# Expert lookup of a PEER layer: sixteen row dots move from VectorE to TensorE, and the expert V rows are split differently

## What is computed

```python
qc = (xc @ w_query).reshape(C, 8, 2, 128)
s = einsum('chpd,hpnd->chpn', qc, sub_keys)          # 128 keys per half
top_s, top_i = top_k(s, 16)
cand_s = top_s[..., 0, :, None] + top_s[..., 1, None, :]
cand_i = top_i[..., 0, :, None] * 128 + top_i[..., 1, None, :]
best_s, best_pos = top_k(cand_s, 16)                 # 16 experts per token and head
expert_idx = take_along_axis(cand_i, best_pos)
g = softmax(best_s)
act = gelu(einsum('chkd,cd->chk', expert_u[expert_idx], xc))
out = einsum('chk,chkd->cd', g * act, expert_v[expert_idx])
```

## Time and profile before

| | us |
|---|---|
| median of three runs | 1690.85 (1689.32 to 1690.89) |
| the profiled execution | 1694.34 |
| its span in the trace | 1692.5 |
| DVE, PE, POOL, ACT busy | 1298.5, 1234.9, 842.8, 460.9 |
| DMA, mean over the span | 340 GB/s |

### The profile page before, as it was taken

One profiled execution on the slowest core, in us unless ns is written; L12 is line 12 of the kernel. 1 busy time (PEld: TensorE's weight loads), 2 busy tenths in 40 slices (PEclk: granted clock), 3 DMA queues, 4 the chain that ended last, 5 costly groups with the idle time before them and its releaser, 6 DMA issues.

```text
span 1692.5 us, 14464 instructions
## 1 busy us (share of the span) xinstructions
PE 1234.9 (73%) x4812; PEld 839.8 (50%) x4812; DVE 1298.5 (77%) x1802; ACT 460.9 (27%) x1023; POOL 842.8 (50%) x546
## 2 busy tenths in 40 slices
PE   9999999999995554001344544454699999999993
PEld 7888887778984343000122322332365555555551
DVE  5554666466699999999999999999796665666667
ACT  5333443554200100000135565552381000000000
POOL 1000010000174888877888888888565443444444
PEclk9999999999997778555666676666699999999997
DMA  8886546348799999999999999999899999999998
GB/s 237 223 207 196 169 143 213 99 148 278 260 410 415 422 411 396 385 371 362 395 382 407 403 413 387 398 401 422 335 313 380 410 409 411 410 410 409 410 409 347
DMA packets 150230, 575.81 MB, mean 340 GB/s; under 512 B 15586, under 2 KB 28596, under 8 KB 117268
## 3 DMA queue, kind: packets, MB, share of 16 engines
q0 software_dynamic: 74384, 421.30, 62.6%
q1 hardware_dynamic: 75460, 152.82, 26.9%
q10 hardware_dynamic: 320, 0.86, 0.1%
HBM read 572.57 MB, written 2.36 MB: 340 GB/s over the span
## 4 chain that ended last, share of the span: by engine, by line
PE 30%; DVE 28%; DMA 24%; POOL 12%; issue 4%; ACT 2%; DVEq 0%; ACTq 0%; POOLq 0%
DMA v_rows<-in_peer_expert_v,pick_row 21%; DVE big L1549 10%; DVE more_rows L1549 8%; PE ps L1692 6%; PE ps L1694 6%; PE ps L1693 6%; POOL big L691 5%; PE ps L2095 4%; POOL more_rows L691 3%; DVE big L1597 3%; POOL v_rows L671 3%; DMA more_rows<-in_peer_expert_u,pick_row 2%; PE ps L2118 1%; DMA big<-in_peer_expert_u,pick_row 1%; DVE big L1574 1%
## 5 line engine op out<-in xcount | busy, mean ns | idle before, releaser
L671 POOL DMA_INDIRECT v_rows<-in_peer_expert_v,pick_row x256 | 307.8, 1202 | 271.7 <-DVE big L1597 234.9
L1597 DVE SCALAR_TENSOR_TENSOR big<-v_rows,pick_w,big 128x1152 f32<-128x1152 f32 x203 | 287.6, 1417 | 151.7 <-DMA v_rows<-in_peer_expert_v,pick_row 149.7
L2095 PE MATMUL ps<-v_rows,diag 128*128 128x512 f32 (+1 forms) x312 | 182.9, 746 | 269.5 <-DMA v_rows<-in_peer_expert_v,pick_row 169.8
L1549 DVE CUSTOM_DVE_ANT_0 big<-big 128x2048 f32<-128x2048 f32 x150 | 340.1, 2283 | 12.9 <-DMA big<-in_peer_expert_u,pick_row 12.5
L691 POOL DMA_INDIRECT big<-in_peer_expert_u,pick_row x150 | 288.8, 1925 | 65.6 <-issue 43.2
L2095 PEld LDWEIGHTS ps<-v_rows,diag 128*128 128x128 f32 x312 | 83.3, 285 | 368.2 <-issue 194.8
L691 POOL DMA_INDIRECT more_rows<-in_peer_expert_u,pick_row x106 | 222.7, 2101 | 75.3 <-issue 28.3
L1030 DVE TENSOR_TENSOR split_lo<-raw,split_hi 128x1024 fp32r<-128x1024 f32 x119 | 145.8, 1225 | 143.7 <-ACT split_hi L719 118.1
L1549 DVE CUSTOM_DVE_ANT_0 more_rows<-more_rows,big 128x2048 f32<-128x2048 f32 x106 | 240.8, 2284 | 11.0 <-DMA more_rows<-in_peer_expert_u,pick_row 11.0
L2127 PE MATMUL ps<-big,dense 128*128 128x512 f32 (+1 forms) x512 | 213.5, 539 | 0.3 <-DMA big<-in_peer_expert_v 0.3
L2127 PE MATMUL ps<-big 128*128 128x512 f32 (+1 forms) x512 | 213.4, 539 | 0.0
(11 more groups left out here) (281 smaller groups left out, 1495.2 us busy)
## 6 DMA issues: line engine op xcount, KB each, us to landing
big<-in_peer_expert_v SPq DMA_DIRECT2D x128, 448.0 KB, 6.8
raw<-in_w_in SPq DMA_DIRECT2D x88, 512.0 KB, 3.7
raw<-in_w_out SPq DMA_DIRECT2D x32, 512.0 KB, 5.1
big<-in_peer_w_query SPq DMA_DIRECT2D x16, 512.0 KB, 6.5
raw<-in_peer_w_query SPq DMA_DIRECT2D x8, 512.0 KB, 7.6
spare<-in_peer_w_query SPq DMA_DIRECT2D x8, 512.0 KB, 8.3
v_rows<-in_peer_expert_v,pick_row POOLq DMA_INDIRECT x256, 14.2
big<-in_peer_expert_u,pick_row POOLq DMA_INDIRECT x150, 9.1
```

Source lines behind the costliest of these rows:

```text
L671: pool.indirect_dma_start(v_row(k), None, v_table, bass.IndirectOffsetOnAxis(pick_row[:, k:k + 1], 0)).then_inc(v_gathered[v_place(k)], 16)
L1549: dve.tensor_tensor_reduce(row, row, XN[:, place_of(m // TOPK)[0], :], 1.0, 0.0, ALU.mult, ALU.add, pick_dot[:, m:m + 1]).then_inc(dotted, 1)
L1597: dve.scalar_tensor_tensor(out=v, in0=row, scalar=pick_w[:, k:k + 1], in1=v, op0=ALU.mult, op1=ALU.add).then_inc(added, 1)
L2095: ins = pe.matmul(psf[:, c:c + w], diag[:, j % DIAGS, :], row[:, c:c + w], start=k == 0, stop=j == pe_adds(PICKS) - 1)
```

## The change

1. **Dots on PE.** Of head steps 1 to 8, the picks k = 4 and k = 10 (`TURNED_DOTS`: 20, 26, 36, 42, ..., 132, 138) are not dotted by DVE. PE turns the row, 16 blocks of 128 x 128, in four groups into two PSUM banks; ACT copies each group into one SBUF buffer (that of the four diagonals, which aren't needed yet); PE multiplies each block with the token columns already turned (`x1t`), into a 128 x 128 square in PSUM. Its diagonal holds the dots. DVE takes it with a product with the identity and a sum over 128 columns (`take_dot`), behind the dot of pick m + 4. The order in which `dotted` counts changes with it (`DOT_ORDER`, `dots_until`). The ring place of such a row is free when it has been turned.
2. **V beside the picks.** `V_FROM` 144 and every third pick, so that row 0 comes at pick 146 in POOL's, ACT's and PE's loops; 37 rows. ACT makes the diagonal ahead of the one-hots of the same m. The ring goes to six places at pick 138.
3. **Columns.** 1088 per gathered V row, 960 in the dense pass (512 + 448 per product pair).
4. **Scores** are made at k = 13 for head steps of the first eight, k = 9 behind them.
5. Small ones: two PSUM banks swapped for the groups, waits that guard PSUM and the diagonal buffer, and four private semaphores replaced by the engine's step counter.

```diff
-U_WIDE = 108
+U_WIDE = 138
-V_ROW = 1152
+V_ROW = 1088
-V_FROM, V_BESIDE = 112, 36
+V_FROM, V_BESIDE = 144, 37
+TURNED_DOTS = [n * TOPK + k for n in range(1, NH + 1) for k in (4, 10)]
+TAKEN_AFTER = 4
+SCORES_AT = (13, 9)
+DOT_GROUPS = 4
+DOT_ORDER = [f for m in range(PICKS) for f in ([m] if m not in TURNED_DOTS else []) + ([m - TAKEN_AFTER] if m - TAKEN_AFTER in TURNED_DOTS else [])]
+DOT_PLACE = {f: i for i, f in enumerate(DOT_ORDER)}
+def dots_until(m):
+    return DOT_PLACE[m] + 1
 def v_until(m):
-    return max(0, m - V_FROM + 1) // 4
+    return max(0, m - V_FROM + 1) // 3
...
                 f = before_in_place(m)
-                if f >= 0:
-                    pool.wait_ge(dotted, f + 1)
+                if f in TURNED_DOTS:
+                    pool.wait_ge(row_turned, DOT_GROUPS * (TURNED_DOTS.index(f) + 1))
+                elif f >= 0:
+                    pool.wait_ge(dotted, dots_until(f))
...
+            def turned_copies(q):
+                for g in range(q * DOT_GROUPS, (q + 1) * DOT_GROUPS):
+                    act.wait_ge(row_turned, g + 1)
+                    if g:
+                        act.wait_ge(turned_used, g)
+                    act.activation(turned_rows.rearrange("p c n -> p (c n)"), ps[:, g % 2, :], ACT.Copy).then_inc(turned_here, 1)
...
+                if m in TURNED_DOTS:
+                    turned_copies(TURNED_DOTS.index(m))
...
+                for p in v_at(m):
+                    pick_diag(p)
                 i = group_at(m)
...
-                for p in v_at(m):
-                    pick_diag(p)
...
+            def take_dot(m):
+                q = TURNED_DOTS.index(m)
+                dve.wait_ge(turned_used, DOT_GROUPS * (q + 1))
+                dots = ps[:, 2 + q % 2, 0:P]
+                dve.tensor_tensor_reduce(dots, dots, ident[:, :], 1.0, 0.0, ALU.mult, ALU.add, pick_dot[:, m:m + 1]).then_inc(dotted, 1)
...
-                pick_dot_of(m)
+                if m not in TURNED_DOTS:
+                    pick_dot_of(m)
+                if m - TAKEN_AFTER in TURNED_DOTS:
+                    take_dot(m - TAKEN_AFTER)
...
+            def turned_dot(m):
+                q, t = TURNED_DOTS.index(m), place_of(m // TOPK)[0]
+                row = row_here(pe, m)
...
+                def turn(c):
+                    g = q * DOT_GROUPS + c
+                    if g >= 2:
+                        pe.wait_ge(turned_here, g - 1)
+                    for j in range(KC // DOT_GROUPS):
+                        k = c * DOT_GROUPS + j
+                        ins = pe.transpose(ps[:, g % 2, j * P:(j + 1) * P], row[:, k * P:(k + 1) * P], ident[:, :])
+                    ins.then_inc(row_turned, 1)
+                def add(c):
+                    if c == 0 and q >= 2:
+                        pe.wait_ge(dotted, dots_until(TURNED_DOTS[q - 2]))
+                    pe.wait_ge(turned_here, q * DOT_GROUPS + c + 1)
+                    for j in range(KC // DOT_GROUPS):
+                        k = c * DOT_GROUPS + j
+                        ins = pe.matmul(ps[:, 2 + q % 2, 0:P], turned_rows[:, j, :], x1t[:, k, t * P:(t + 1) * P], start=k == 0, stop=k == KC - 1)
+                    ins.then_inc(turned_used, 1)
+                turn(0)
+                for c in range(1, DOT_GROUPS):
+                    turn(c)
+                    add(c - 1)
+                add(DOT_GROUPS - 1)
...
-                if k == TOPK - 1 and n + 2 < HEADS:
+                if k == SCORES_AT[n // NH] and n + 2 < HEADS:
                     head_scores(n + 2)
...
                 i = group_at(m - 2)
                 if i is not None:
                     group(0, i)
+                if m in TURNED_DOTS:
+                    turned_dot(m)
```

More of the change, by code:

```diff
@@ L414, in layer @@
         query_used = sem("query_used")
+        row_turned, turned_here, turned_used = sem("row_turned"), sem("turned_here"), sem("turned_used")
+        turned_rows = diag[:, :, :]
+        ALL_TURNED = DOT_GROUPS * len(TURNED_DOTS)
         def query_name(n):
@@ L940, in hot_first @@
                     v = hot0[:, 1, j, :]
-                    act.activation(v, iota[:, :], ACT.Square, bias=picks_t[:, 1, token:token + 1], scale=-1.0).then_inc(sem("hot_squared"), 1)
-                    act.wait_ge(sem("hot_squared"), token + 1)
+                    link(act.activation(v, iota[:, :], ACT.Square, bias=picks_t[:, 1, token:token + 1], scale=-1.0))
                     act.activation(v, v, ACT.Relu, bias=1.0, scale=-1.0).then_inc(sem("hot_act"), 1)
@@ L960, in group_out @@
                 act.wait_ge(token_made, t * P + (i + 1) * GROUP_TOKENS)
+                if t == 0 and i == 0:
+                    act.wait_ge(turned_used, ALL_TURNED)
                 act.activation(dense_w[t][:, :, i * GROUP_TOKENS:(i + 1) * GROUP_TOKENS],
-                               ps[:, 3 + i % 2, :].rearrange("p (j a) -> p a j", j=GROUP_TOKENS), ACT.Copy).then_inc(group_moved, 1)
+                               ps[:, 4 - i % 2, :].rearrange("p (j a) -> p a j", j=GROUP_TOKENS), ACT.Copy).then_inc(group_moved, 1)
+            def turned_copies(q):
[4 more added lines that the diff above has]
+                    act.activation(turned_rows.rearrange("p c n -> p (c n)"), ps[:, g % 2, :], ACT.Copy).then_inc(turned_here, 1)
             for m in range(PICKS):
@@ L1006, in _ @@
             v = slice(V_ROW, V_ROW + CHUNK)
-            act.activation(X[:, 1, v], ps[:, 6, :], ACT.Copy).then_inc(sem("dense_copied"), 1)
-            act.wait_ge(sem("dense_copied"), 1)
+            link(act.activation(X[:, 1, v], ps[:, 6, :], ACT.Copy))
             act.dma_start(out_rows[:, 1, v], X[:, 1, v]).then_inc(out_stored, 16)
@@ L1625, in _ @@
             after()
-            dve.tensor_tensor(pick_exp[:, 0:TOPK], head_best, head_best[:, 0:1].broadcast_to([P, TOPK]), ALU.subtract).then_inc(sem("first_exp"), 1)
+            step(dve.tensor_tensor(pick_exp[:, 0:TOPK], head_best, head_best[:, 0:1].broadcast_to([P, TOPK]), ALU.subtract))
             first_rows(1, TOPK)
-            dve.wait_ge(sem("first_exp"), 1)
+            after()
             dve.wait_ge(sem("first_rows"), 2)
@@ L2106, in group @@
             def group(t, i):
+                if t == 0 and i == 1:
+                    pe.wait_ge(dotted, dots_until(TURNED_DOTS[-1]))
                 if t * GROUPS + i >= 2:
@@ L2117, in group @@
                     hot = hot1[:, i % SEAM_HOT, :, j, :] if t else hot0[:, :, j, :]
-                    pe.matmul(ps[:, 3 + i % 2, j * P:(j + 1) * P], hot[:, 1, :], hot[:, 0, :], start=True, stop=True).then_inc(token_made, 1)
+                    pe.matmul(ps[:, 4 - i % 2, j * P:(j + 1) * P], hot[:, 1, :], hot[:, 0, :], start=True, stop=True).then_inc(token_made, 1)
             def dense(a):
```

10 lines of the change are left out of this document (7 added, 3 removed).

## The result

The changed kernel takes 1681.35 us (median of 7, 1678.41 to 1683.42) against 1690.89 for the kernel before in the same runs: a ratio of 0.9937 (95% interval 0.9922 to 0.9951), which is 10.7 us of 1690.89 (the two medians are 9.5 apart). The forecast was 1680.

The account below looks back on a forecast made before the run. Bound: picks shared among DVE, DMA and POOL, dense pass by full PE and DMA. Pick 144 at 847 + 340 + seam 75.2 + dense 413.8 + tail 5.3 = 1681.3 us span, 1680 as run median; range 1666 to 1696.

Parts of the forecast that it names:

- The turned dots: Picks 48 to 138: DVE falls to 39.4 us per head, DMA's 39.7 becomes the limit; TensorE's chain of 11 us hidden.
- missed gathers: Picks 48 to 138: 0.9 us per head added for gathers that miss their gap in DVE's work, 5 us in all.
- the narrowing of the ring: At pick 138 instead of 108: gather 138 waits for pick 134's dot, DMA briefly runs dry; 5 us (0 to 10).
- The third limit: In the picks, POOL gets about one gather per dot, one more for a DVE gap over some 1.2 us.
- V at every third pick: Picks 144 to 255: 37 V rows instead of 28; nine more gathers cost 8 us (0 to 21), stretch 340 us.
- Diagonals ahead of the one-hots: Last stretch of the picks: removes PE's wait for ACT, said to be on nobody's path; priced at nothing.
- The seam: Between picks and dense pass: 21 adds of 1.41 us get 5.6% narrower, 1.6 us less (0 to 2), 75.2 us.
- The dense pass and the end: Dense pass 27.4 us longer, 413.8; V done 402 us after its start, PE last; 5.3 us behind PE.
- Gathers never bind: Rival, picks: turned stretch at DMA's floor, nine V rows cost 2 us; kernel time 1664 us, chance 0.11.
- One gather per dot: Rival, picks: fewer openings for POOL, 45 us per head with both gap gathers missed; kernel time 1718 us, chance 0.14.
- V didn't end last: Rival, dense pass: V still ends last, 425 us from the start instead of 419; kernel time 1686 us, chance 0.11.
- no turned dot came late: Rival, picks: turned dots come late, DVE waits some 3 us at some five; kernel time 1695 us, chance 0.07.

Follow-up runs that it names:

- the plain sums: Changed kernel with each VectorE dot of 2048 columns replaced by a plain sum of the row, one SBUF input instead of two: 1664.7 us, ratio 0.9841.

## Why the prediction was right

By its own terms, from the profiled executions:

| step | forecast | measured |
|---|---|---|
| start of pick 48 | 598.5 | 600.9, in a run whose dots began 1.8 us later |
| pick 48 to 144 | 248.5 | 242.4 |
| pick 144 to the seam | 340 | 347.4 |
| seam | 75.2 | 71.1 |
| dense pass | 413.8 | 414.4 |
| behind PE | 5.3 | 5.4 |

*The turned dots.* Pace, cause and limit were as forecast: DVE down by 1.9 us per dot, DMA at 420 GB/s, two dots enough to reach it. Of the 10 us that were added for missed gathers and for the narrowing of the ring, some 4 were used (242.4 us for 96 picks, where 2.48 us each make 238); the other 6 are what the stretch was shorter by. Gathers that begin inside a dot still end 0.9 us after it, but DVE idles 4 us per 160 here; that this is what lets POOL catch up was not tried by itself.

*Gathers per dot.* The third limit, read from the timeline of the kernel before, was real, and the plain sums show its cause. The Trainium skill's inference (SBUF — State Buffer, § Who interferes with whom) that descriptor generation is spared by a DVE instruction with two SBUF inputs doesn't hold for these gathers: 2.10 us a gather beside the dots with two inputs, 0.99 beside the sums with one, and the V adds and one-hots, which are no custom instructions, hold them as the dots do. Its rule that an instruction with one SBUF input leaves GpSimd alone agrees with the second number.

*V at every third pick.* The price was undersized: 15 us against 8, between the bounds of 0 and 21. The prediction took 8 us for nine gathers on the ground that some of them would lie in DVE's idle time: each in fact cost 1.6 us, two thirds of a gather's 2.37, and DVE's waits for landings rose from 11 us to 27.5 instead of shrinking.

*Diagonals ahead of the one-hots.* "On nobody's path here: at nothing" was wrong as a price of the edit. At every third pick the change needs it, 18 us, and the forecast came out because the edit was made. For V rows at every fourth pick nothing here tries it by itself: the kernel before, with late diagonals, took 327.8 us for the last stretch, and the changed one with every fourth V row and early diagonals 328.3. The rows that should have warned are these waits of the kernel before, from pick 144 to the seam (us, times, longest):

```profile
PE ps L2095 <- ACT diag L917: 97.3, 16, 8.9
DVE big L1574 <- PE ps L2118: 4.9, 3, 2.1
```

It looks like the same loop, just starting to close.

*The seam.* 1.6 us were forecast and 5.7 came. Kernels with V at every third pick have 75 to 78 us from the last dot to the dense pass, those with every fourth 80 to 82, whatever the columns. So it goes with that edit; what in it does so was not tried. (The forecast also counted 21 adds where the trace of before has 24 in the seam, which makes 0.2 us.)

*The dense pass and the end.* 27.4 forecast, 28.0 measured; PE last, as forecast. But the last V add ended 395 us after the start instead of 402, so PE was alone for 19 us rather than 12. The 12 us stood in the prediction's own sum and were the hint that the split had gone too far.

*The rivals.* "Gathers never bind" is what the plain sums give: 1664.7 us, where 1664 was worked out for it, but pick 144 came 3 us later than in its sum and the way from there to the dense pass took 402 us instead of 409, so part of that closeness is chance. "One gather per dot" priced two missed gaps; none was missed for good. V didn't end last, and no turned dot came late.

So the forecast came out 1 us off (1680 against 1681.35) though the measured steps were 2, 7 and 1 us longer than forecast and 6 and 4 shorter. Apart from the price of the diagonals' place the mechanisms were right; that the sum came out so close is in part luck.

## What to carry to other kernels

When an engine that both computes and frees buffers is relieved, price what it feeds: here DMA's limit took two dots per head and not a third, and the issue of gathers on GpSimd took back part of the rest. Where two streams end side by side, read which one is last and by how much before moving work between them: the slack of the other (19 us here) is the most that can be moved. And before an edit of order is priced at nothing, look for a loop of waits over three engines that it opens or closes; a small wait in it at one rate becomes the bound at the next.

## What the runs showed of the hardware

A gather's issue on GpSimd (0.94 us by itself) that begins inside a VectorE instruction with two operands out of SBUF ends 0.81 to 0.87 us after that instruction: a custom dot, a SCALAR_TENSOR_TENSOR or a TENSOR_TENSOR alike. Beside a sum of the same 2.28 us with one such operand, or an addition of 1088 columns out of PSUM, it takes 0.93 to 1.00 us.

The time of DMA packets does not grow evenly with their size. In 340 us in the middle of the dense pass the mean gathered packet took 172.3 ns with 4352 bytes (1088 columns), 173.2 with 4480, 176.6 with 4544 and 181.9 with 4608; the mean dense one 144.3 ns with 3584 bytes, 143.6 with 3648, 145.2 with 3712 and 153.7 with 3840. These are the packets of rows alone, by their size in the traces. The queues below also hold packets of 4 bytes, one to every eight of rows, of 9 to 10 ns, so the mean of a whole queue is lower. The kernel after (packets, MB, share of 16 engines' 340 us; 0.635 × 16 × 340 us over all 22382 packets is 154 ns):

```profile
q0 software_dynamic: 22382, 86.60, 63.5%
q1 hardware_dynamic: 15215, 51.98, 38.5%
```

And with 1120 + 928 columns:

```profile
q0 software_dynamic: 22607, 90.03, 64.4%
q1 hardware_dynamic: 15733, 51.93, 37.6%
```

So 4480 and 3712 bytes (1120 and 928 columns) took 1 ns more than packets 128 bytes smaller, and 8 to 9 ns less than packets 128 bytes larger, and that split moved 420 GB/s instead of 410. With 4544 and 3648 bytes it was 416; whether the sizes or the addresses within a row make the difference was not tried.
